# Rotary scores over 128 rows with zero-padded query tiles, and two smaller edits at the norms, in a two-layer encoder kernel

## What is computed

```python
for i in range(DEPTH):                      # 2
    y = rmsnorm(h, attn_norm_g[i])
    y = conv_module(y, ...) if i == 0 else mla(y, ...)
    h = h + y
    h = h + swiglu(rmsnorm(h, ffn_norm_g[i]), ...)
return rmsnorm(h, final_norm_g)

# conv_module: pointwise product to 4096 channels, gate, depthwise convolution of
# 31 taps, then this norm and one more pointwise product
v = jax.nn.silu(layernorm(v, ln_g, ln_b))
return v @ w_pw2 + b_pw2

# mla: 16 heads, 128 channels without rotation and 64 rotary ones
s = (jnp.einsum('bqhd,bkhd->bhqk', q_nope[:, q0:kend], k_nope[:, :kend])
     + jnp.einsum('bqhr,bkr->bhqk', q_rope[:, q0:kend], k_rope[:, :kend]))
```

## Time and profile before

| | us |
|---|---|
| median of 3 runs | 2124.07 |
| lowest and highest | 2123.80, 2124.23 |
| the profiled execution's own time | 2124.01 |
| its span in the trace | 2122.2 |
| what lies around the span | 1.8 |

### The profile page before, as it was taken

One profiled execution on the slowest core, in us unless ns is written; L12 is line 12 of the kernel. 1 busy time (PEld: TensorE's weight loads), 2 busy tenths in 40 slices (PEclk: granted clock), 3 DMA queues, 4 the chain that ended last, 5 costly groups with the idle time before them and its releaser, 6 DMA issues.

```text
span 2122.2 us, 25267 instructions
## 1 busy us (share of the span) xinstructions
PE 2082.7 (98%) x9810; PEld 1747.1 (82%) x9810; DVE 1284.3 (61%) x1568; ACT 790.8 (37%) x727; POOL 20.8 (1%) x23
## 2 busy tenths in 40 slices
PE   6999999999999999999999999999999999999997
PEld 6888878888888888888888888888888888888886
DVE  2999986555555555555566665465555555555555
ACT  3000263433333333333344444353333333333343
POOL 0000000000000000000001000000000000000001
PEclk9999999999999999999999999999999999999999
DMA  6444446555556555565545434656556555565551
GB/s 205 158 146 152 139 156 204 192 186 196 182 194 195 183 195 185 191 198 182 194 139 149 139 119 146 210 180 197 182 189 201 182 195 185 190 198 182 194 191 67
DMA packets 219728, 374.91 MB, mean 177 GB/s; under 512 B 17180, under 2 KB 58916, under 8 KB 219172
## 3 DMA queue, kind: packets, MB, share of 16 engines
q1 hardware_dynamic: 218256, 370.76, 53.9%
q10 hardware_dynamic: 1428, 3.55, 0.5%
HBM read 372.18 MB, written 2.10 MB: 176 GB/s over the span
## 4 chain that ended last, share of the span: by engine, by line
PE 94%; DVE 3%; ACT 1%; issue 1%; DMA 0%; SPq 0%; DVEq 0%; ACTq 0%
PE ps L1139 90%; DVE scratch L803 2%; PE ps L1291 1%; PE ps L1473 1%; PE ps L1472 1%; DMA scratch<-in_conv_b_dw_dram 0%; PE ps L1453 0%; PE ps L1183 0%; PE ps L1172 0%; DVE resid L967 0%; ACT scratch L635 0%; ACT w_hi L435 0%; PE ps L1454 0%; DVE x_lo L724 0%; SPq L318 0%
## 5 line engine op out<-in xcount | busy, mean ns | idle before, releaser
L697 DVE TENSOR_TENSOR w_lo<-raw,w_hi 128x2048 fp32r<-128x2048 f32 x321 | 734.8, 2292 | 605.3 <-ACT w_hi L435 604.4
L435 ACT ACTIVATE w_hi<-raw 128x2048 fp32r<-128x2048 f32 x321 | 614.2, 1918 | 876.5 <-PE ps L1139 863.1
L1139 PE MATMUL ps<-w_hi,x_hi 128*128 128x512 f32 x1728 | 675.2, 391 | 1.4 <-DVE x_lo L724 1.0
L1139 PE MATMUL ps<-w_hi,x_lo 128*128 128x512 f32 x1728 | 672.7, 389 | 0.0
L1139 PE MATMUL ps<-w_lo,x_hi 128*128 128x512 f32 x1728 | 672.3, 389 | 0.0
L1139 PEld LDWEIGHTS ps<-w_hi,x_hi 128*128 128x128 f32 x1728 | 324.4, 188 | 69.3 <-DVE x_lo L724 1.5
L1139 PEld LDWEIGHTS ps<-w_hi,x_lo 128*128 128x128 f32 x1728 | 324.4, 188 | 67.6
L1139 PEld LDWEIGHTS ps<-w_lo,x_hi 128*128 128x128 f32 x1728 | 324.5, 188 | 66.5
L1139 PE MATMUL ps<-w_hi,a_hi 128*128 128x512 f32 (+1 forms) x768 | 292.3, 381 | 2.4 <-DVE a_lo L944 2.4
L1139 PE MATMUL ps<-w_hi,a_lo 128*128 128x512 f32 (+1 forms) x768 | 292.0, 380 | 0.0
L1139 PE MATMUL ps<-w_lo,a_hi 128*128 128x512 f32 (+1 forms) x768 | 292.0, 380 | 0.0
(11 more groups left out here) (175 smaller groups left out, 888.3 us busy)
## 6 DMA issues: line engine op xcount, KB each, us to landing
raw<-in_ffn_w_gate_dram SPq DMA_DIRECT2D x88, 1024.0 KB
raw<-in_ffn_w_up_dram SPq DMA_DIRECT2D x88, 1024.0 KB
raw<-in_ffn_w_down_dram SPq DMA_DIRECT2D x88, 1024.0 KB
raw<-in_conv_w_pw_dram SPq DMA_DIRECT2D x64, 512.0 KB
raw<-in_conv_w_pw_dram SPq DMA_DIRECT2D x16, 1024.0 KB
raw<-in_mla_w_o_dram SPq DMA_DIRECT2D x16, 1024.0 KB
raw<-in_mla_w_ukv_dram SPq DMA_DIRECT2D x8, 1024.0 KB
raw<-in_mla_w_dq_dram SPq DMA_DIRECT2D x4, 1024.0 KB
```

The source lines that it names most:

```text
L435: act.activation(w_hi[:, slot, :], raw[:, slot, :], ACT.Copy).then_inc(hi_done, 1)
L697: dve.tensor_tensor(w_lo[:, g % RING, :], raw[:, g % RING, :], hi32(w_hi[:, g % RING, :]), ALU.subtract).then_inc(lo_dve, 1)
L1139: ins = pe.matmul(dst, lhsT, rhs, start=first and n == 0, stop=last and n == len(pairs) - 1, skip_group_check=skip)
```

## The change

1. **Small loads.** All small loads but `freq` (nine, so `SMALL = 9`) are issued by ScalarE, ahead of its other work; SP issues none of them. `freq` goes to SP's queue behind the second half's weight loads and has a semaphore of its own.
2. **First norm.** ScalarE squares token tile 0 alone and VectorE all of tile 1; one addition on VectorE goes.
3. **Last statistics of the convolution.** VectorE reads them from PSUM as soon as TensorE is done, and ScalarE's copy to `ytmp` waits until they are taken. The last 512 columns of the normalising wait for those copies.
4. **Rotary scores.** VectorE writes each head's rotary queries into a plane of its own of `qr_pad`, whose other 64 partitions GpSimd has set to zero once at the start. The second matmul of each score runs over all 128 rows, with the whole `krT`. One addition of 128 x 256 on VectorE becomes two of 64 x 256, each with its own count on `qr_done`.

```diff
@@ first_norm, ScalarE and VectorE
-                act.wait_ge(x_in[1], 16)
-                act.activation(ytmp[:, 1, D // 2:], resid[:, 1, D // 2:], ACT.Square, accum_out=ssq[:, 1, 0:1]).then_inc(sq_act, 1)
...
-                link(dve.tensor_tensor_reduce(out=ytmp[:, 1, 0:D // 2], in0=resid[:, 1, 0:D // 2], in1=resid[:, 1, 0:D // 2],
-                                              scale=1.0, scalar=0.0, op0=ALU.mult, op1=ALU.add, accum_out=stat[:, 1:2]))
-                dve.wait_ge(sq_act, SQ[0])
-                link(dve.tensor_tensor(stat[:, 1:2], stat[:, 1:2], ssq[:, 1, 0:1], ALU.add))
-                mean_square(SQ[0], D)
-                inv_sqrt().then_inc(rstd_ready, 1)
+                square_sum(0)
@@ SP
             for s in range(HALVES):
                 pw1_loads(s)
+                if s == 1:
+                    sp.dma_start(freq[:, :], inv_freq).then_inc(freq_in, 16)
@@ GpSimd
+            for a in range(2):
+                pool.memset(qr_pad[ROPE * (1 - a):ROPE * (2 - a), a, :], 0.0).then_inc(qr_zero, 1)
@@ rows_out, ScalarE
                     act.wait_ge(conv_tr, TT * s + t + 1)
+                    if s == HALVES - 1:
+                        act.wait_ge(last_stats, t + 1)
@@ row_stats, VectorE
-                    dve.wait_ge(row_done, TT * s + t + 1)
-                    last = dve.bn_stats(bn[:, t, s, :], ytmp[:, t, CH // 2 * s:CH // 2 * (s + 1)])
+                    if s < HALVES - 1:
+                        dve.wait_ge(row_done, TT * s + t + 1)
+                        src = ytmp[:, t, CH // 2 * s:CH // 2 * (s + 1)]
+                    else:
+                        dve.wait_ge(conv_tr, TT * s + t + 1)
+                        src = ps[:, 4 + 2 * (s % 2) + t, 0:CH // 2]
+                    last = dve.bn_stats(bn[:, t, s, :], src)
@@ pair_queries, VectorE
-                dve.tensor_tensor(qrT, rope_a, rope_b, ALU.add).then_inc(qr_done, 1)
+                for a in range(2):
+                    r = slice(ROPE * a, ROPE * a + ROPE)
+                    dve.tensor_tensor(qr_pad[r, a, :], rope_a[r, :], rope_b[r, :], ALU.add).then_inc(qr_done, 1)
@@ pair_scores, TensorE
-                pe.wait_ge(qr_done, val(h + 1, i, 2))
...
+                    pe.wait_ge(qr_done, val(2 * h + a + 1, i, 4))
...
-                        ins = pe.matmul(ps[:, 4 + a, cols], qrT[r, toks], krT[r, 0:keys], start=False, stop=True)
+                        ins = pe.matmul(ps[:, 4 + a, cols], qr_pad[:, a, toks], krT[:, 0:keys], start=False, stop=True)
```

More of the change, by code:

```diff
@@ L82 @@
 R_ALL = 120
+SMALL = 9
 PI_DIGITS = 314159265358979323846264338327950288419716939937510582097494
@@ L134, in encoder @@
         bias1_col = sb("bias1_col", [P, 2 * KT])
+        qr_pad = sb("qr_pad", [P, 2, S])
         rlat = sb("rlat", [P, 2])
@@ L172, in encoder @@
         q_raw = scratch[:, 1536:1792]
-        qrT = scratch[:, 1792:2048]
         prob = scratch[:, 2048:2816].rearrange("p (a f) -> p a f", a=2)
@@ L198, in encoder @@
         small_in = sem("small_in")
+        freq_in = sem("freq_in")
         bias2_in = sem("bias2_in")
@@ L225, in encoder @@
         conv_tr = sem("conv_tr")
+        last_stats = sem("last_stats")
         z_done = sem("z_done")
@@ L240, in encoder @@
         swaps = sem("swaps")
+        qr_zero = sem("qr_zero")
         q_raw_done = sem("q_raw_done")
@@ L279, in small_inputs @@
                     (vec_row[R_KVN:R_KVN + LT, :], rows(mla_kv_norm_g[0])), (bias1_row, rows(conv_b_pw1[0])),
-                    (tap_row, conv_w_dw[0].rearrange("w (t p) -> (w t) p", p=P).rearrange("(q r) p -> r q p", q=4)),
-                    (freq[:, :], inv_freq)]
+                    (tap_row, conv_w_dw[0].rearrange("w (t p) -> (w t) p", p=P).rearrange("(q r) p -> r q p", q=4))]
         block = ctx.enter_context(nc.Block())
@@ L300, in _ @@
             x_t = x[0].rearrange("(t p) d -> p t d", p=P)
-            small = small_inputs()
             for t in range(TT):
@@ L316, in pw1_loads @@
                         if s == 0 and j == 1 and h == 0:
-                            for n in range(len(small) // 2):
-                                sp.dma_start(*small[n]).then_inc(small_in, 16)
-                            sp.wait_ge(small_in, 16 * 10)
+                            sp.wait_ge(small_in, 16 * SMALL)
                         sp.dma_start(dst[:, :, h, :], w1[:, GK * j:GK * j + GK, h, CH // 2 * s:CH // 2 * (s + 1)]
@@ L395, in _ @@
                                pattern=[[-1, P]], channel_multiplier=1).then_inc(consts, 1)
+            pool.wait_ge(consts, 2)
+            for a in range(2):
+                pool.memset(qr_pad[ROPE * (1 - a):ROPE * (2 - a), a, :], 0.0).then_inc(qr_zero, 1)
             pool.wait_ge(rstd_ready, RSTD[3])
+            pool.wait_ge(qr_zero, 2)
             half = ROPE // 2
@@ L421, in _ @@
         def _(act):
-            small = small_inputs()
-            for n in range(len(small) // 2, len(small)):
-                act.dma_start(*small[n]).then_inc(small_in, 16)
+            for dst, src in small_inputs():
+                act.dma_start(dst, src).then_inc(small_in, 16)
             act.wait_ge(consts, 2)
@@ L509, in _ @@
             for c in range(CC):
+                if c == CC - 1:
+                    act.wait_ge(row_done, TT * HALVES)
                 act.activation(ytmp[:, 0, CH * c:CH * c + CH], ytmp[:, 0, CH * c:CH * c + CH], ACT.Identity,
@@ L810, in row_stats @@
                 for t in range(TT):
-                    dve.wait_ge(row_done, TT * s + t + 1)
-                    last = dve.bn_stats(bn[:, t, s, :], ytmp[:, t, CH // 2 * s:CH // 2 * (s + 1)])
-                return last
+                    if s < HALVES - 1:
[5 more added lines that the diff above has]
+                    last = dve.bn_stats(bn[:, t, s, :], src)
+                    if s == HALVES - 1:
+                        last.then_inc(last_stats, 1)
             for s in range(HALVES):
                 conv_half(s)
-            link(row_stats(HALVES - 1))
+            row_stats(HALVES - 1)
+            dve.wait_ge(last_stats, TT)
             for t in range(TT):
@@ L824, in _ @@
             for c in range(CC):
+                if c == CC - 1:
+                    dve.wait_ge(row_done, TT * HALVES)
                 dve.tensor_scalar(ytmp[:, 1, CH * c:CH * c + CH], ytmp[:, 1, CH * c:CH * c + CH], mv[:, 1, 0:1],
@@ L848, in rope_angle @@
                 dve.wait_ge(pos_in, 16)
+                dve.wait_ge(freq_in, 16)
                 link(dve.tensor_copy(pos_f, pos_i.bitcast(I32)))
@@ L1185, in residual_transposes @@
                     ins.then_inc(x_tr, 1)
-            pe.wait_ge(small_in, 16 * 10)
+            pe.wait_ge(small_in, 16 * SMALL)
             pe.wait_ge(consts, 2)
@@ L1505 @@
 RSTD = {0: 1, 2: 3, 3: 4, 5: 7, 6: 8}
-SQ = {0: 2, 2: 3, 3: 4, 5: 7}
+SQ = {0: 1, 2: 2, 3: 3, 5: 6}
 AHI = {0: 0, 1: 2 * FC + 2 * LT}
```

2 lines of the change are left out of this document (1 added, 1 removed).

## The result

| | before | after |
|---|---|---|
| median, us | 2124.15 (2123.80 to 2124.63, 4 runs) | 2111.55 (2110.78 to 2112.02, 4 runs) |
| profiled execution, us | 2124.01 | 2112.02 |
| its span, us | 2122.2 | 2110.2 |

The ratio of the new time to the old is 0.994, with a 95% interval from 0.9923 to 0.9957: 12.6 us less. The forecast was 2112.8, 11.2 less. The profiled execution of the changed kernel was the slowest of its four, so the two spans differ by only 12.0 us. These 12.0 us split at places that both chains have: +0.23 up to the first product, -0.41 at the end of the convolution, -0.14 between the two, and -11.7 behind the convolution's norm, where the attention is.

What follows compares the result with a forecast made beforehand. TensorE's own work was taken to bound the kernel, at 94% of the span. 2124.0 - 11.0 (scores) - 0.4 (convolution's end) + 0.2 (start) = 2112.8 us, range 2109.0 to 2115.0.

Steps and rivals of the forecast that it cites:

- The scores' block: A pair's eight score products on TensorE: 2.60 us in place of 3.98, products at 0.22 and 0.43 throughout.
- rival B: Scores: the excess comes from alternating operands or from adding to a bank, and stays; 2123.8 us, 6%.
- The eighth passage: From a pair's 64-row scores back to the next 128-row projections: between 0 and 0.1 us, taken as 0.
- VectorE's cover: The extra VectorE addition per pair costs 0, with 1.5 us of cover; without cover 0.4 us a pair.
- the term of -11.0: Gain at the scores: 8 pairs x 1.38 us = 11.0 us, up to 11.9 with the eighth passage.
- The end of the convolution: Statistics start without ScalarE's copy ahead of them: -0.4 us, from -0.45 to -0.2.
- The allowance of 0.4 us for the clock: End of the convolution: an earlier start may meet the clock's rise at another point, +-0.4 us.
- The start: TensorE's first work waits for the last small load; moving loads gives +0.2 us, the new norm alone 0.
- The two opposite terms of the sum: Start: 112 rows ahead of the taps, up to +2.0 us; freq no longer waited for, 0 to -2 us.
- A: Scores: two heads' 64-row matmuls already overlap, and padding takes that away; slower, 2129.0 us, 4%.
- C: Start: the taps' issue is held until near 15 us, so x is ready later; +4, 2116.8 us, 8%.
- D: Start: the small loads land early and the norm sets the start; -2.7 us, 2109.9 us, 20%.

Runs made afterwards that it cites:

- run 4: run 2 with one index changed, so the second head's rotary products take the first head's 64 rows too: 2114.49 us.
- run 7: The kernel before with only the convolution's last statistics read from PSUM beside ScalarE's copy: 2124.27 us.
- run 1: The kernel before with only the zero-padded rotary queries and their 128-row products: 2112.55 us.
- run 2: The kernel before, rotary products left at 64 rows, a pair's four 128-row products first and its four 64-row ones behind, head by head: 2110.51 us.
- run 3: run 2 with the four grouped 64-row products alternating between the two heads: 2109.46 us.
- run 8: The kernel before with only the small loads moved to ScalarE's queue and freq to SP's: 2124.22 us.
- run 9: The changed kernel with the taps' load issued as two loads, of 112 and 12 partitions: 2108.41 us.
- run 11: The kernel before with run 2's grouped 64-row products, statistics from PSUM, moved small loads with taps cut, new norm, no padding: 2105.64 us.

## Why the prediction was right, and where it was off

The median came out at 2111.55 us for a forecast of 2112.8. Between the two profiled executions the gain is 12.0 us for a forecast of 11.2, and the scores make up 0.7 of the difference.

**The scores' block: right.** Forecast 2.60 us a block and 0.22 and 0.43 throughout; measured 2.62. The reading of the 0.20 us as the price of a passage, and not of accumulation or of operands (rival B), is shown by the padded block and by run 4, where one passage into the 64-row group costs 0.20 and one out of it 0.20.

**The eighth passage: mis-sized.** The prediction took 0 for the passage back to the projections, with 0.1 as its bound. It costs what the others do: 10.27 - 10.07 = 0.20 us a pair, 1.6 us in all, twice the bound. The prediction leaned on a first product that takes longer behind any float32 block, and that is no measure of the passage: a float32 block stands ahead of the projections in the changed kernel too, and the 0.20 comes on top of what it costs.

**VectorE's cover: wrong at one pair.** "Cost 0, with 1.5 us of cover" compared VectorE's addition with the time at which TensorE wanted it before the change. With TensorE 1.4 to 1.6 us earlier in each pair, and VectorE in that stretch not held by TensorE, the cover at the second pair was gone: 0.74 us. The row it rested on, was even read at the second pair, the very one that failed; what was missing was the question what that row hangs on. That VectorE fits into the shorter pair was read from the earlier trace rows, a later pair with two remainders of weights; the stretch that leads to the second addition has four. From the third pair on VectorE has that room again.

So the term of -11.0 was in truth 8 x (1.36 + 0.20) = 12.5, less 0.74: -11.7, which is what the two spans show. The two misses had opposite signs. That 11.7 lies between the 11.0 and 11.9 of the forecast is luck in that sense: the passages alone come to 12.5, above its bound. The range was also added up unevenly: the text gives the convolution -0.8 to +0.2, the two sums take -0.4 and 0.0; with the bounds themselves it would be 2108.6 to 2115.2, and the result lies inside either.

**The end of the convolution: right.** Forecast -0.4, measured -0.41 in the changed kernel and -0.42 in run 7. Reading PSUM cost VectorE nothing more (0.43 us, as before). The allowance of 0.4 us for the clock was not needed. The granted clock rose earlier in the changed kernel, before the stretch from 272 to 274 us:

```profile
272.00:274.00 2.00, 2.00 (x12) 2.00 (x11) 0.91 (x2) 1.97 (x5) 0.00 (x0) 0.50 0.00 0
```

```profile
272.00:274.00 2.00, 1.56 (x15) 1.32 (x13) 1.12 (x2) 1.97 (x5) 0.00 (x0) 1.00 0.00 0
```

The first is before, the second after; the columns are those of the earlier trace rows, and the clock is the 0.50 (1.2 GHz) and the 1.00 (2.4 GHz). TensorE at the full level is idle for a part of the stretch, ScalarE is busy 1.97 of 2.00 us in both, and the second product comes no sooner than the earlier end of the statistics gives. The transposes wait for ScalarE there, not for the clock.

**The start: right in sum, by luck.** Forecast +0.2, measured +0.23 at the first product. Only 0.04 of it is the landing; most of the rest is the transposes, 5.60 us against 5.42. Both numbers come from single traces. The six traces with the old loads and the old norm (the kernel before and runs 1, 2, 3, 4 and 7) have TensorE's first instruction anywhere from 16.33 to 17.26 and the first product from 22.80 to 24.30, so +0.23 can't be told from nothing, and neither can the 0.12 of the moved loads alone (run 8) from my 0.2 or from the 0 that the rule of the Trainium skill gave (DMA: Bandwidth & Descriptors, Issuing engines are not separate DMA queues).

The two opposite terms of the sum can be seen in the packets of ScalarE's queue. The taps' rows of 512 bytes end at 15.10 us in the kernel before, with packets of 4 bytes, as those of `freq` are, behind them until 16.07; in the changed kernel the rows end at 15.92 with nothing to wait for behind them. That the taps are the long load was right. The estimate that 50 to 80 rows a microsecond set their landing was right for this form of the load only: cut in two, the same number of rows landed 3.4 us earlier.

**The rivals.** A did not happen, and its mechanism exists: in the kernel before, the 64-row products stood apart and nothing overlapped, so padding lost nothing. Its rule in the Trainium skill (TensorEngine Tiling (Array Packing), Theoretical Speedup) holds for products in different halves with no 128-row product between them: 0.65 us in place of 1.30. The same page of the Trainium skill (Tiling Modes, Key Properties) says that a change of the tiling mode drains TensorE; the runs put a price on it here, 0.20 us each way. B fell with the first block. C fell: the table load began at 5.69, where C had it near 15. D did not happen in this change, but run 9 made it happen, with its price short by 0.7 us: -2.7 forecast, -3.4 at the first product (20.14 against 23.58). The prediction let the small vectors take 1.3 us up to the transposes of x, and the earlier trace rows has 18.16 - 16.44 = 1.72. From 18.16 the bound of 15.0 is -3.2; the transposes came at 14.81, another -0.2, and took 5.33 in place of 5.42.

## What to carry to other kernels

Count the changes between 64-row and 128-row matmuls in TensorE's order, the one into the next block too: each cost 0.20 us here. Before padding half tiles, try putting those of different halves into one group with no full one between them. That kept one change in and one out here, and halved the time of the products.

When an edit shortens the engine that sets the pace, measure the cover of every other engine against the new time, and do it for the round in which the other engine has most to do. Here that was the stretch to the second pair, with four weight groups for VectorE in place of two. A load that lands late may be late for its shape: 124 partitions in one load took 3.4 us longer than 112 and 12 in two.

## What was not expected of the hardware

- Four 64-row float32 products in different halves of the rows took 0.65 us in one group and 1.30 us when both heads lay in the same half. The order of the heads in the group made no difference, and TensorE started a product ahead of one that stands before it in the program.
- The transposes of x at the start take 4.4 to 5.9 us from run to run of nearly the same code (4.44 in run 11, 5.88 in run 2). They start 0.21 us apart and then, from some moment on, 0.11. In all 14 traces that moment is, within 0.1 us, the first entry in the trace's record of the granted clock, at the full level of 2.4 GHz: 21.98 us in the kernel before, 22.39 in the changed one, 22.80 in run 2, 20.16 in run 3. Ahead of it the record has no entry, and the views print 1.00 there. That TensorE ran at the other level, 1.2 GHz, until then is read from the pace alone, 0.21 being twice 0.11. The moment lies 3.5 to 6.5 us behind TensorE's first instruction, and what sets it within these bounds stays open. It moves the time by up to 1.4 us, more than the edits of the start and of the convolution together.
